# Attention stage of a two-block model: gate products ahead of modulation sums, a softmax in three parts with its maximum as ACT's bias, the output product in two halves, and two norms from one chain

## Chip, cores and metric

One NeuronCore of one Trainium2 chip runs the whole program. The metric is device time in microseconds (us) of the execution, lower is better.

## The reference

Two model blocks run one after the other on 256 tokens of 1024 channels, float32. The first (RWKV and mLSTM mixing, then a mixture of experts) ends in a norm; the second takes its result. The change lies where they meet and in the second block's attention:

```python
x = x + g_f * y                                   # end of block 1
x = rms_norm(x, final_norm_w)
# block 2, layer 0
mod = silu(c) @ w + b; shift, scale, gate = split(mod, 3)
h = rms_norm_2(x, norm_w) * (1.0 + scale) + shift
proj = h @ w_in                                   # gq gk gv gg glr sq sk sv
o_gla = gla_chunked(gq, gk, gv, log_a)            # 4 heads, chunks of 64
o_gla = rms_norm_2(o_gla, gla_norm_w) * silu(gg)
s = einsum(q, k) * 0.125 + bias                   # 8 heads, window 128, 2 blocks of 128 queries
m = maximum(max(s), sink)
p = exp(s - m); p = p / (sum(p) + exp(sink - m))
o_swa = einsum(p, v)
x = x + gate * (concatenate([o_gla, o_swa]) @ w_out)
# then norm, modulation and a squared-relu MLP of 4096; a second layer; final norm
```

`rms_norm(x, w)` is `x * rsqrt(mean(x*x) + 1e-6) * w`.

## The kernel before

The program is written engine by engine: each engine has one queue of instructions in the order of its function, and waits on counting semaphores. So the order of work around the change is the order in which the code is written. `Counter.link` lets an instruction count up a semaphore and then has its own engine wait for it; `mark` only counts up. The table `STEP` names counts, and `x.wait_ge(v["bs"], STEP["bs.sub0"])` waits for such a point (`v`, `a`, `g`, `t` are DVE, ACT, POOL and PE).

**Where block 1 ends.** `scatter` is the last expert product. DVE adds it to `x_sb` for each half of the tokens (`tt` 0 and 1, `v_residual`). Then for each half ACT squares and sums a row (L470), DVE makes the mean (L500), POOL raises it to the power -0.5 (L466) and DVE scales `x_sb` by root and weight (`final`, L2033). On the scaled row the same four steps are done again for block 2's norm, whose last one (L508) writes `xn`. PE transposes `xn` (L592), and DVE (L545) and ACT (L490) write the modulated `hT`. Then PE starts on the projections (L2699, the rank-16 gate).

**Projections and the gated linear attention.** `projection(0)` to `projection(8)` (L2687 to L2693) take 256 columns of `w_in` each, and 8 banks of PSUM are shared: projection i writes bank 6 + i % 2. Projections 4 and 5 give the output gate `gg`; ACT writes its sigmoid, and DVE multiplies it by the value still in the bank (L2098). `projection(6)` and `(7)` write the same two banks and wait for these two products. Between them PE makes the chunk states' sums (`bg.ds`, L2737) and the outputs (`bg.o`, L2749, L2752); DVE carries the state over the chunks in 12 small instructions (L2090, L2091).

**The modulation stream.** The vectors of the next modulation come from 24 pieces of `ada_w_2`, 0.5 MB each. SP loads piece n into one of four slots once DVE has used piece n - 4 (L745). `mod1_step` (L1165 for a vector's first piece, L1168) adds one piece to a sum on DVE. Pieces 0 to 7 make one vector, 8 to 15 the next, 16 to 23 the last; PE's `finish` sums over the partitions. Between the pieces SP also loads the four quarters of the output weight (L767, 1 MB each). All of it goes through one queue.

**Softmax and output.** PE makes the scores into six banks (L2770): two banks for the first 128 queries (`sc[:, :, 0:P]`), four for the second (two key blocks). DVE scales and adds the bias (L2134, L2141), and in `under_maximum` takes the maximum over a row (L2125), the maximum with the sink (L2126), their difference (L2127) and subtracts the maximum from all scores (L2128). ACT applies the exponential (L1515), PE transposes the weights (L2782), ACT copies them (L1519), PE multiplies by the values (L2789, L2791), DVE divides (L2155) into `y2`. PE transposes `y2` (L2801; channels 0 to 511 are the linear attention, 512 to 1023 the softmax attention), ACT copies a rounded part (L1539), DVE the rest (L578). The output product `mm3` (L573) then takes three passes for each product of 128x512: rounded by rounded, rounded by rest, rest by rounded. The weight is split in the same way: `out_hi_copy` (L1509) on ACT, `trailing` for the rest, its first three quarters on POOL (L1041), the fourth on DVE. After 96 products in four banks, block 2's next norm (`l0`) and the MLP follow.

## Time and profile before

| | |
|---|---|
| three runs, us | 1256.24, 1245.6, 1258.23 |
| median, us | 1256.24 |
| the profiled execution, us | 1254.31 |
| its span from first to last instruction, us | 1252.6 |
| busy share of the span: PE, DVE, ACT, POOL | 85%, 51%, 28%, 14% |
| mean granted clock of TensorE | 0.922 |

The busy shares are averages over stages with different limits. The change touches the stretch from 636 to 816 us of the profiled span, a seventh of it. There PE is the engine on which all others hang, and what is to be read is which wait of PE's ends last.

### The profile page before, as it was taken

Reading aid. Unit: us, or ns where it says so; the run is one execution under the profiler, and the core shown is the slowest. Engines: PE = TensorE matmul, PEld = TensorE weight load, DVE = VectorE, ACT = ScalarE, POOL = GpSimd, SP = SyncE. Lnnn points to the kernel's source line nnn. Section 1 sums busy time; section 2 is a strip of 40 time slices with the busy share of each in tenths; the row PEclk is TensorE's granted clock in tenths of the full one; section 3 lists DMA queues with packets and bytes.
Section 4 is the critical chain, followed back from the end, with each engine's and each line's share of the span. In section 5 each row is a group of like instructions: output and inputs, shape, how many; then the busy total and the mean of one; then the engine's idle time right before and its main releaser. Section 6 shows DMA issues by size and latency. Waiting matters only on the chain.

```text
span 1252.6 us, 16197 instructions
## 1 busy us (share of the span) xinstructions
PE 1070.0 (85%) x6588; PEld 814.6 (65%) x6588; DVE 640.0 (51%) x812; ACT 351.5 (28%) x440; POOL 178.0 (14%) x234
## 2 busy tenths in 40 slices
PE   1898977999978899999539794979999976999995
PEld 1787844997535455555227683858888865888884
DVE  6565567646444333323045727376757467553433
ACT  1130024241111111111023105166354315543531
POOL 4701013000200133231011004011111130000000
PEclk9998987999977999999869997889999977999998
DMA  9979638204679999999979703056676461545510
GB/s 352 351 163 307 242 123 305 102 1 169 228 305 408 383 401 353 356 339 355 407 226 371 277 1 135 1 203 251 235 294 225 134 247 73 192 144 194 225 67 34
DMA packets 114090, 287.48 MB, mean 230 GB/s; under 512 B 16406, under 2 KB 42334, under 8 KB 114026
## 3 DMA queue, kind: packets, MB, share of 16 engines
q1 hardware_dynamic: 94514, 245.45, 52.6%
q10 hardware_dynamic: 7560, 26.74, 6.3%
q0 software_dynamic: 11952, 14.38, 3.8%
q8 instruction: 46, 0.75, 0.2%
q14 instruction: 18, 0.15, 0.0%
HBM read 334.23 MB, written 2.62 MB: 269 GB/s over the span
## 4 chain that ended last, share of the span: by engine, by line
PE 68%; DMA 13%; DVE 10%; SPq 3%; ACT 2%; issue 2%; POOL 1%; DVEq 0%; ACTq 0%; POOLq 0%
PE ps L573 29%; PE ps L2245 6%; PE ps L2582 5%; DMA arena<-in_moe_w_down_dram 4%; PE ps L2561 4%; PE ps L2421 3%; DMA macc<-in_ada_w_dram 3%; PE ps L2609 3%; DMA ring<-in_w_in_dram 2%; PE ps L2508 2%; PE ps L2687 2%; SPq L763 1%; PE ps L2624 1%; DMA ring<-in_ada_w_dram 1%; SPq L619 1%
## 5 line engine op out<-in xcount | busy, mean ns | idle before, releaser
L578 DVE TENSOR_TENSOR ring_parts<-ring,arena_parts 128x2048 fp32r<-128x2048 f32 x65 | 146.6, 2286 | 49.1 <-ACT arena_parts L1109 42.1
L573 PE MATMUL ps<-arena_parts,macc_parts 128*128 128x512 f32 x512 | 166.0, 396 | 0.0
L573 PE MATMUL ps<-arena_parts,gate_parts 128*128 128x512 f32 x288 | 114.6, 398 | 8.3 <-DVE hT_parts L578 8.3
L573 PE MATMUL ps<-ring_parts,gate_parts 128*128 128x512 f32 x288 | 113.5, 394 | 0.0
L573 PE MATMUL ps<-arena_parts,hT_parts 128*128 128x512 f32 x288 | 113.4, 394 | 0.0
L573 PEld LDWEIGHTS ps<-arena_parts,macc_parts 128*128 128x128 f32 x512 | 96.2, 188 | 19.6
L573 PE MATMUL ps<-ring_parts,macc_parts 128*128 128x512 f32 x256 | 99.8, 390 | 0.0
L1109 ACT CAST arena_parts<-ring 128x2048 fp32r<-128x2048 f32 x32 | 60.3, 1908 | 84.5 <-DMA ring<-in_mlp_w_dram 43.4
L2245 PE MATMUL ps<-hT,ring 128*128 128x256 f32 x288 | 70.1, 409 | 5.6 <-DMA ring<-in_w_in_dram 5.6
L2245 PEld LDWEIGHTS ps<-hT,ring 128*128 128x128 f32 x288 | 59.5, 208 | 15.3 <-DMA ring<-in_w_in_dram 6.0
L573 PEld LDWEIGHTS ps<-arena_parts,gate_parts 128*128 128x128 f32 x288 | 55.1, 191 | 20.5 <-DVE hT_parts L578 9.1
L2582 PE MATMUL ps<-ring,hT 128*32 128x256 f32 x1024 | 61.7, 387 | 5.3 <-issue 3.4
L466 POOL TENSOR_TENSOR small<-small,nhalf 128x1 f32<-128x1 f32 x16 | 10.0, 625 | 390.1 <-DVE small L500 390.0
L573 PEld LDWEIGHTS ps<-arena_parts,hT_parts 128*128 128x128 f32 x288 | 55.0, 191 | 11.7
L573 PEld LDWEIGHTS ps<-ring_parts,gate_parts 128*128 128x128 f32 x288 | 55.1, 191 | 11.3
L1089 ACT CAST arena_parts<-ring 128x2048 fp32r<-128x2048 f32 x32 | 60.0, 1911 | 5.3 <-DMA ring<-in_mlp_w_dram 5.2
L578 DVE TENSOR_TENSOR macc_parts<-ps,macc_parts 128x512 fp32r<-128x512 f32 x32 | 22.1, 691 | 75.9 <-ACT macc_parts L1133 75.9
L2012 DVE SCALAR_TENSOR_TENSOR macc_parts<-ps,small,macc_parts 128x512 fp32r<-128x512 f32 x24 | 16.9, 747 | 85.8 <-ACT macc_parts L1439 85.8
L1572 DVE SCALAR_TENSOR_TENSOR macc<-ring,ccol,macc 128x1024 f32<-128x1024 f32 x42 | 54.0, 1285 | 8.5 <-DMA ring<-in_ada_w_dram 7.1
L2582 PEld LDWEIGHTS ps<-ring,hT 128*32 128x32 f32 x1024 | 34.3, 112 | 33.9 <-issue 13.5
L2609 PE MATMUL ps<-arena,gate 128*32 128x512 f32 x384 | 45.6, 607 | 10.8 <-DMA arena<-in_moe_w_down_dram 9.5
L573 PEld LDWEIGHTS ps<-ring_parts,macc_parts 128*128 128x128 f32 x256 | 48.2, 188 | 9.3
(539 smaller groups left out, 1799.0 us busy)
## 6 DMA issues: line engine op xcount, KB each, us to landing
ring<-in_mlp_w_dram SPq DMA_DIRECT2D x40, 1024.0 KB, 7.6
arena<-in_moe_w_down_dram SPq DMA_DIRECT2D x16, 2048.0 KB, 12.4
ring<-in_ada_w_dram SPq DMA_DIRECT2D x29, 1024.0 KB, 13.4
ring<-in_mlp_w_dram ACTq DMA_DIRECT2D x24, 1024.0 KB, 7.1
ring<-in_moe_w_up_dram SPq DMA_DIRECT2D x10, 2048.0 KB, 22.3
ring<-in_moe_w_gate_dram SPq DMA_DIRECT2D x10, 2048.0 KB, 17.8
arena<-in_ada_w_dram SPq DMA_DIRECT2D x15, 1024.0 KB, 7.0
ring<-in_w_in_dram SPq DMA_DIRECT2D x13, 1024.0 KB, 18.4
```

What stands on the lines that cost most here:

```text
L573: ins = nc.tensor.matmul(o, l, r, start=start and i == 0, stop=stop and i == 2, skip_group_check=True)
L578: return eng.tensor_tensor(lo, x, hi.bitcast(F32), ALU.subtract)
L1089: nc.scalar.copy(mlp_hi[s_], ring[:, s_, :]).then_inc(a_w2, 1)
L1109: nc.scalar.copy(mlp_hi[s_], ring[:, s_, :]).then_inc(a_w1, 1)
L1572: ins = nc.vector.scalar_tensor_tensor(acc, w[:, r, :], ccol[:, k:k + 1], acc, ALU.mult, ALU.add)
L2245: ins = nc.tensor.matmul(o, w[:, k, P * j:P * j + P], hT[:, k, :], start=k == 0, stop=k == KT - 1)
L2421: ins = nc.tensor.matmul(o, lhs[:, gi, hh], rhs[:, gi, hh], start=True, stop=True)
L2508: ins = nc.tensor.matmul(ps[:, 4 + j, :], hT[:, k, P * (j // 2):P * (j // 2) + P], w, start=k == 0, stop=k == KT - 1)
L2561: ins = nc.tensor.matmul(ps[:, 6 + i // 2, 256 * (i % 2):256 * (i % 2) + 256], xn[:, tt, P * k:P * k + P], picked[:, tt, :], start=tt == 0 ...
L2582: ins = nc.tensor.matmul(ps[rows, 4 + i % 2, FE * half:FE * half + FE], hT[:, k, P * (i % 2) + CAPQ * j:P * (i % 2) + CAPQ * j + CAPQ], w[ ...
L2609: ins = nc.tensor.matmul(ps[rows, 6 + h, :], tb[:, P * f + CAPQ * j:P * f + CAPQ * j + CAPQ], down_w[:, j, f, 512 * h:512 * h + 512], star ...
L2687: ins = nc.tensor.matmul(o, w[:, k, P * j:P * j + P], hT[:, k, :], start=k == 0, stop=k == KT - 1)
```

## The change

Five edits, engine by engine. `order` shows what each engine's queue holds; line numbers after the change are larger, up to 100 by the end.

**Norms.** Where block 1 meets block 2, `x_sb` is multiplied by the weight alone (`weighted`, into `xn`), and both sums of squares are taken beside each other, of `x_sb` and of `xn`. With v = mean(x²)+1e-6 and w2 = mean((x·w)²) the second norm's factor on x·w is (w2 + 1e-6·v)^-0.5, so that its chain does not need the root of v; that root is used for `x_sb` alone, whose scaling (`final_out`) now comes behind `hT`. POOL:

```diff
+g_rstd(pool, cn, "bn", 0)
+g_rstd(pool, cn, "bn", 1)
 for tt in range(TT):
-    g_rstd(pool, cf, "f", tt)
-    g_rstd(pool, cn, "bn", tt)
+    pool.wait_ge(v["f"], STEP[f"f.ss{tt}"])
+    cf.link(nc.gpsimd.tensor_tensor(f_var[tt], f_var[tt], nhalf[:, 0:1], ALU.pow))
+    cf.at(f"f.rstd{tt}")
```

The three subtractions of the weight's rest part leave POOL, and DVE has them behind the linear attention:

```diff
-for q in range(3):
-    pool.wait_ge(a["bs"], STEP[f"bs.hi{q}"])
-    c.link(trailing(nc.gpsimd, ring_lo[:, (9 + q) % RING, :], ring[:, (9 + q) % RING, :], out_hi[q]))
-c.at("bg.lo")
```

```diff
+for q in range(3):
+    dve.wait_ge(a["bs"], STEP[f"bs.hi{q}"])
+    c.link(trailing(nc.vector, ring_lo[:, (9 + q) % RING, :], ring[:, (9 + q) % RING, :], out_hi[q]))
+c.at("bg.lo")
```

ACT, the squares, and then its queue from projection 4 on:

```diff
-    a_square(cf, "f", tt)
-    act.wait_ge(v["f"], STEP[f"f.n{tt}"])
-    a_square(cn, "bn", tt)
+    cf.link(nc.scalar.activation(sq_out[tt], x_sb[:, tt, :], ACT.Square, accum_out=f_var[tt]))
+    cf.at(f"f.sq{tt}")
+    act.wait_ge(v["f"], STEP[f"f.w{tt}"])
+    cn.link(nc.scalar.activation(sq_out[tt], xn[:, tt, :], ACT.Square, accum_out=small[:, tt:tt + 1]))
+    cn.at(f"bn.sq{tt}")
...
 for i in range(4, 9):
     if i == 6:
         act.wait_ge(t_fin, FIN[1, 2])
     copied(i)
+    if i == 6:
+        act.wait_ge(t["bg"], STEP["bg.o"])
+        out_hi_copy(0)
+        act.wait_ge(v["bg"], STEP["bg.ss"])
+        out_hi_copy(1)
+    elif i == 7:
+        act.wait_ge(v["bg"], STEP["bg.y"])
+        out_hi_copy(2)
 cp.at("bp.a")
-
-c = Counter(act, a["bs"])
-
-def out_hi_copy(q):
-    act.wait_ge(ring2[(9 + q) % RING], 32)
-    c.link(nc.scalar.copy(out_hi[q], ring[:, (9 + q) % RING, :]))
-    c.at(f"bs.hi{q}")
+nc.scalar.activation(swm[:, 48:49], ones[:, 0:1], ACT.Exp)
 
 def exp_part(part):
     act.wait_ge(v["bs"], STEP[f"bs.sub{part}"])
-    s_ = sc[:, :, P * part:P + 2 * P * part]
-    c.link(nc.scalar.activation(s_, s_, ACT.Exp))
+    for i in range(8 if part == 0 else 4):
+        h = i + 4 * (part == 2)
+        s_ = sc[:, h, 0:P] if part == 0 else sc[:, h, P:3 * P]
+        m = i + (0, 8, 12)[part]
+        c.mark(nc.scalar.activation(s_, s_, ACT.Exp, bias=swm[:, m:m + 1]))
...
+ch = Counter(act, a["bo"])
+
+def out_t(k):
+    act.wait_ge(t["bo"], k // 2 + 1)
+    ch.link(nc.scalar.copy(gT_hi[:, k:k + 2, :], ps[:, k // 2, :].rearrange("p (k t) -> p k t", k=2)))
+
+for k in (0, 2):
+    out_t(k)
 exp_part(0)
-c.at("bs.exp0")
-for j in range(2):
+exp_part(1)
+for j in (0, 1):
     weights_t(j)
-out_hi_copy(2)
-exp_part(1)
+c.at("bs.pt0")
+exp_part(2)
 c.link(nc.scalar.activation(swm[:, 16:32], swm[:, 16:32], ACT.Exp))
-c.at("bs.exp1")
+c.at("bs.es")
 for j in range(2, 6):
     weights_t(j)
 c.at("bs.pt")
 out_hi_copy(3)
-c = Counter(act, a["bo"])
-for k in range(0, KT, 2):
-    act.wait_ge(t["bo"], k // 2 + 1)
-    c.link(nc.scalar.copy(gT_hi[:, k:k + 2, :], ps[:, k // 2, :].rearrange("p (k t) -> p k t", k=2)))
+for k in (4, 6):
+    out_t(k)
```

DVE's norms:

```diff
+def weighted(tt):
+    c.link(nc.vector.tensor_tensor(xn[:, tt, :], x_sb[:, tt, :], nrm_b, ALU.mult))
+    c.at(f"f.w{tt}")
+
+def final_var(tt):
+    dve.wait_ge(a["f"], STEP[f"f.sq{tt}"])
+    c.link(nc.vector.tensor_scalar(f_var[tt], f_var[tt], 1.0 / D, EPS, ALU.mult, ALU.add))
+    c.at(f"f.ss{tt}")
+    c.link(nc.vector.tensor_scalar(f_eps[tt], f_var[tt], EPS, None, ALU.mult))
+
+def both_var(tt):
+    dve.wait_ge(a["bn"], STEP[f"bn.sq{tt}"])
+    cn.link(nc.vector.scalar_tensor_tensor(small[:, tt:tt + 1], small[:, tt:tt + 1], 1.0 / D, f_eps[tt],
+                                           ALU.mult, ALU.add))
+    cn.at(f"bn.ss{tt}")
+
+def both_out(tt):
+    dve.wait_ge(g["bn"], STEP[f"bn.rstd{tt}"])
+    cn.link(nc.vector.tensor_scalar(xn[:, tt, :], xn[:, tt, :], small[:, tt:tt + 1], None, ALU.mult))
+    cn.at(f"bn.xn{tt}")
+
+def final_out(tt):
     dve.wait_ge(g["f"], STEP[f"f.rstd{tt}"])
-    c.link(nc.vector.scalar_tensor_tensor(x_sb[:, tt, :], x_sb[:, tt, :], small[:, tt:tt + 1], nrm_b,
-                                          ALU.mult, ALU.mult))
-    c.at(f"f.n{tt}")
+    c.link(nc.vector.scalar_tensor_tensor(x_sb[:, tt, :], x_sb[:, tt, :], f_var[tt], nrm_b, ALU.mult, ALU.mult))
...
-final(0)
+weighted(0)
+final_var(0)
 v_residual(dve, c, "f", gate1[:, 1, :], 0, 1, experts_of)
-v_mean(dve, cn, "bn", 0)
-v_mean(dve, c, "f", 1)
-v_xn(dve, cn, "bn", 0)
-final(1)
-v_mean(dve, cn, "bn", 1)
-v_xn(dve, cn, "bn", 1)
+weighted(1)
+both_var(0)
+final_var(1)
+both_out(0)
+both_var(1)
+both_out(1)
 v_norm_out(dve, cn, "bn", *mod_of[0])
+final_out(0)
+final_out(1)
+c.at("f.n1")
```

DVE's stream (the first `mod1_step` group of eight stays where it was):

```diff
-for n in range(8, 11):
-    mod1_step(dve, n)
...
-for n in range(11, 17):
+for n in range(8, 14):
     mod1_step(dve, n)
...
-for n in range(17, 24):
+for n in range(14, 19):
     mod1_step(dve, n)
...
 cp = Counter(dve, v["bp"])
 for i in (4, 5):
     dve.wait_ge(a["bp"], i + 1)
     gs = ggs[:, :, 256 * (i - 4):256 * (i - 4) + 256]
     cp.link(nc.vector.tensor_tensor(gs, gs, bin_bank(i).rearrange("p (a n) -> p a n", a=2), ALU.mult))
+for n in range(19, 24):
+    mod1_step(dve, n)
+
 dve.wait_ge(t["bg"], STEP["bg.o"])
```

DVE's softmax and the rest parts of `y2`:

```diff
+parts = ((0, sc[:, :, 0:P], 0), (8, sc[:, 0:4, P:3 * P], 0), (12, sc[:, 4:8, P:3 * P], 4))
+
+def under_maximum(o, s_, h0):
+    n = s_.shape[1]
+    m, e, s0 = mx[:, o:o + n], es[:, o:o + n], slice(h0, h0 + n)
+    c.link(nc.vector.tensor_reduce(m, s_, AX_X, ALU.max))
+    c.link(nc.vector.scalar_tensor_tensor(m, m, -1.0, nsink[:, s0], ALU.mult, ALU.min))
+    c.link(nc.vector.tensor_tensor(e, sink_b[:, s0], m, ALU.add))
 
...
+    if j % 2:
+        under_maximum(*parts[j // 2])
+        c.at(f"bs.sub{j // 2}")
...
+def out_lo(cb, k):
+    dve.wait_ge(a["bo"], k // 2 + 1)
+    cb.link(trailing(nc.vector, hT_lo[:, k:k + 2, :], ps[:, k // 2, :].rearrange("p (k t) -> p k t", k=2),
+                     gT_hi[:, k:k + 2, :]))
+
+cb = Counter(dve, v["bo"])
+for k in (0, 2):
+    out_lo(cb, k)
+dve.wait_ge(a["bs"], STEP["bs.es"])
+for o, s_ in ((0, sc[:, :, 0:P]), (8, sc[:, :, P:3 * P])):
     c.link(nc.vector.tensor_reduce(dn[:, o:o + 8], s_, AX_X, ALU.add))
...
-c = Counter(dve, v["bo"])
-for k in range(0, KT, 2):
-    dve.wait_ge(a["bo"], k // 2 + 1)
-    c.link(trailing(nc.vector, hT_lo[:, k:k + 2, :], ps[:, k // 2, :].rearrange("p (k t) -> p k t", k=2),
-                    gT_hi[:, k:k + 2, :]))
+c = cb
+for k in (4, 6):
+    out_lo(c, k)
```

PE from the scores on:

```diff
+def out_products(k0):
+    for j in range(4):
+        for k in range(k0, k0 + 4):
+            if j == 0 and k % 2 == 0:
+                pe.wait_ge(v["bo"], k // 2 + 1)
+            cols = slice(D * (k % 2) + 512 * (j % 2), D * (k % 2) + 512 * (j % 2) + 512)
+            tok = slice(P * (j // 2), P * (j // 2) + P)
+            ins = mm3(ps[:, 4 + j, :], gT_hi[:, k, tok], hT_lo[:, k, tok], out_hi[k // 2][:, cols],
+                      ring_lo[:, (9 + k // 2) % RING, cols], start=k == 0, stop=k == KT - 1)
+        if k0:
+            ins.then_inc(t_bout, 1)
+
+pe.wait_ge(v["bg"], STEP["bg.y"])
+out_transposes(0)
...
-    if j in (0, 2):
+    if j % 2 == 0:
         pe.wait_ge(a["bs"], STEP[f"bs.exp{j // 2}"])
...
+pe.wait_ge(a["bs"], STEP["bs.pt0"])
+for h in range(SWA_H):
+    kv = slice(64 * (h // 4), 64 * (h // 4) + 64)
+    ins = nc.tensor.matmul(ps[:, 2, 64 * h:64 * h + 64], p_t[:, h, :], svt[:, 0, kv], start=True, stop=True)
+c.mark(ins)
+c.at("bs.o0")
...
+pe.wait_ge(v["bg"], STEP["bg.lo"])
+out_products(0)
 pe.wait_ge(v["bs"], STEP["bs.y"])
+out_transposes(4)
+out_products(4)
```

DVE at the end of the chunk states. Before (L2090 and L2091 are the state, L2098 the gate products, L2101 to L2103 take the linear attention's output), and then after the change, where L2138 are the gate products and L1170 the stream's steps:

```order
L2090 TENSOR_TENSOR arena<-arena 64x2x128
L2091 TENSOR_TENSOR arena<-arena,ps 64x2x128
L2098 TENSOR_TENSOR arena<-arena,ps 128x2x256 x2
L2101 COPY macc<-ps 128x2x512
L2102 TENSOR_TENSOR arena<-macc 128x1024
L2103 TENSOR_REDUCE small<-arena 128x8
```

```order
L2131 TENSOR_TENSOR arena<-arena 64x2x128
L2132 TENSOR_TENSOR arena<-arena,ps 64x2x128
L2138 TENSOR_TENSOR arena<-arena,ps 128x2x256 x2
L1170 SCALAR_TENSOR_TENSOR wup<-gate,ccol,wup 128x1024
L1170 SCALAR_TENSOR_TENSOR wup<-macc,ccol,wup 128x1024 x2
L1170 SCALAR_TENSOR_TENSOR wup<-gate,ccol,wup 128x1024 x2
L2144 COPY macc<-ps 128x2x512
L2145 TENSOR_TENSOR arena<-macc 128x1024
```

Five steps of the stream, which stood ahead of the state, now stand behind the gate products.

PE from the scores (L2770, after it L2825) to the output product. Before, with the softmax's weights transposed in L2782, the products with the values in L2789 and L2791, and all of `y2` in L2801:

```order
L2770 MATMUL ps<-arena 128x128 x8
L2770 MATMUL ps<-arena 128x256 x8
L2782 MATMUL ps<-ident,arena 128x128 x24
L2789 MATMUL ps<-arena 128x64
L2791 MATMUL ps<-arena 128x64 x2
```

```order
L2791 MATMUL ps<-arena 128x64 x2
L2801 MATMUL ps<-ident,macc 128x128 x16
L573 MATMUL ps<-arena_parts,gate_parts 128x512
L573 MATMUL ps<-ring_parts,gate_parts 128x512
L573 MATMUL ps<-arena_parts,hT_parts 128x512
```

After it, with `y2` in L2836, the weights in L2860 and the values in L2867 and L2874:

```order
L2825 MATMUL ps<-arena 128x128 x8
L2825 MATMUL ps<-arena 128x256 x8
L2836 MATMUL ps<-ident,macc 128x128 x8
L2860 MATMUL ps<-ident,arena 128x128 x24
L2867 MATMUL ps<-arena 128x64 x8
L2874 MATMUL ps<-arena 128x64 x16
L576 MATMUL ps<-arena_parts,gate_parts 128x512
L576 MATMUL ps<-ring_parts,gate_parts 128x512
L576 MATMUL ps<-arena_parts,hT_parts 128x512
```

Half of the transposes of `y2` moved ahead of those of the softmax, and the output product's first half directly behind the products with the values; the other half of the transposes stands behind its 48th instruction.

ACT from projection 6 on. Before (L1464 and L1468 copy projections, L1509 rounds the weight, L1515 is the exponential, L1519 copies the transposed weights):

```order
L1464 COPY arena<-ps 128x512 x2
L1468 COPY arena<-ps 64x256 x4
L1469 COPY arena<-ps 128x256
L1509 CAST arena_parts<-ring 128x2048 x2
L1515 ACT_TABLE_LOAD
L1515 ACTIVATE arena<-arena 128x8x128
L1519 COPY arena<-ps 128x512 x2
L1509 CAST arena_parts<-ring 128x2048
L1515 ACTIVATE arena<-arena 128x8x256
```

After it (L1507 rounds the weight, L1531 is the exponential, L1542 copies the transposed `y2`):

```order
L1468 COPY arena<-ps 128x512
L1507 CAST arena_parts<-ring 128x2048 x2
L1468 COPY arena<-ps 128x512
L1507 CAST arena_parts<-ring 128x2048
L1472 COPY arena<-ps 64x256 x4
L1473 COPY arena<-ps 128x256
L1523 ACT_TABLE_LOAD
L1523 ACTIVATE arena<-ones 128x1
L1542 CAST gate_parts<-ps 128x512 x2
L1531 ACTIVATE arena<-arena 128x128 x8
L1531 ACTIVATE arena<-arena 128x256 x4
L1536 COPY arena<-ps 128x512 x2
```

Three roundings moved up between the copies of projections, the table load ahead of the softmax, and two instructions became sixteen, with two copies of `y2` ahead of them.

## Rows read from the trace of the kernel before

**Rows 1.** Windows: start:end, length, busy us per engine, PEclk, DMA share, GB/s.

```profile
684.00:711.00 27.00, 26.86 (x133) 22.34 (x131) 22.10 (x22) 4.92 (x8) 0.00 (x0) 1.00 0.98 376
776.00:790.00 14.00, 11.71 (x64) 11.12 (x64) 7.61 (x7) 4.24 (x5) 2.08 (x1) 0.62 0.00 0
790.00:816.00 26.00, 25.98 (x119) 22.16 (x120) 8.87 (x14) 4.01 (x7) 0.54 (x1) 0.93 0.00 1
```

**Rows 2.** Timeline of PE: start us, busy us, line, operation, idle before and releaser.

```profile
656.40 5.51 PE L2699 MATMUL ps<-hT,arena 128*16 128x256 f32 x16 [1.72 <-DVE hT L545]
...
703.68 7.17 PE L2689 MATMUL ps<-ring,hT 128*128 128x256 f32 x32
718.73 8.61 PE L2687 MATMUL ps<-hT,ring 128*128 128x256 f32 x32 [7.87 <-DVE arena L2098]
...
753.53 5.51 PE L2770 MATMUL ps<-arena 128*128 128x128 f32 x32 [2.11 <-ACT arena L1469]
...
780.40 0.43 PE L2789 MATMUL ps<-arena 128*128 128x64 f32 x2 [0.73 <-ACT arena L1519]
...
790.02 3.58 PE L2801 MATMUL ps<-ident,macc 128*128 128x128 f32 x16 [1.58 <-DVE macc L2155]
...
815.24 1.04 PE L592 MATMUL ps<-ident,arena 128*128 128x128 f32 x8
```

**Rows 3.** Timeline, the same columns: ACT in the two norms.

```profile
639.13 1.06 ACT L470 ACTIVATE arena<-x_sb 128x1024 f32<-128x1024 f32 x1 [6.91 <-DVE x_sb L517]
...
642.71 1.06 ACT L470 ACTIVATE arena<-x_sb 128x1024 f32<-128x1024 f32 x1 [2.42 <-DVE x_sb L2033]
...
645.61 1.06 ACT L470 ACTIVATE arena<-x_sb 128x1024 f32<-128x1024 f32 x1 [1.75 <-DVE x_sb L517]
...
649.69 1.06 ACT L470 ACTIVATE arena<-x_sb 128x1024 f32<-128x1024 f32 x1 [2.94 <-DVE x_sb L2033]
```

**Rows 4.** Timeline of DVE beside the modulation stream, 677 to 713 us.

```profile
677.61 1.42 DVE L2059 TENSOR_TENSOR_SCAN arena<-early,arena 128x256 f32<-128x256 f32 x2
...
698.39 0.75 DVE L1165 TENSOR_SCALAR wup<-macc,ccol 128x1024 f32<-128x1024 f32 x1 [2.48 <-DMA macc<-in_ada_w_dram]
...
711.26 1.28 DVE L1168 SCALAR_TENSOR_TENSOR wup<-gate,ccol,wup 128x1024 f32<-128x1024 f32 x1 [0.49 <-DMA gate<-in_ada_w_dram]
712.47 0.41 DVE L2090 TENSOR_TENSOR arena<-arena 64x256 f32<-64x256 f32 x1
```

**Rows 5.** Source line 745, the stream's pieces: from issue to landing.

```profile
DMA to landing us min/median/max: 3.7/6.5/11.5
```

**Rows 6.** Timeline of DVE and then POOL in the softmax.

```profile
754.82 0.69 DVE L2134 SCALAR_TENSOR_TENSOR arena<-ps,arena 128x512 f32<-128x512 f32 x1 [10.83 <-PE ps L2770]
...
756.41 1.22 DVE L2125 TENSOR_REDUCE arena<-arena 128x8 f32<-128x1024 f32 x1
757.67 2.44 DVE L2126 TENSOR_TENSOR arena<-arena 128x8 f32<-128x8 f32 x1
...
760.34 5.41 DVE L2128 TENSOR_TENSOR arena<-arena 128x1024 f32<-128x1024 f32 x1
...
771.00 0.17 DVE L2126 TENSOR_TENSOR arena<-arena 128x8 f32<-128x8 f32 x1
...
782.38 2.29 DVE L578 TENSOR_TENSOR ring_parts<-ring,arena_parts 128x2048 fp32r<-128x2048 f32 x1 [2.30 <-ACT arena_parts L1509]
...
755.55 9.12 POOL L578 TENSOR_TENSOR ring_parts<-ring,arena_parts 128x2048 fp32r<-128x2048 f32 x2 [17.44 <-ACT arena_parts L1509]
```

**Rows 7.** Timeline of ACT, gate bias, exponentials and copies.

```profile
670.17 0.98 ACT L1479 ACTIVATE arena<-ps,prm_c 128x256 f32<-128x256 f32 x2 [0.48 <-PE ps L2705]
...
765.83 1.28 ACT L1515 ACT_TABLE_LOAD   x1 [8.49 <-DVE arena L2128]
...
773.79 1.91 ACT L1515 ACTIVATE arena<-arena 128x2048 f32<-128x2048 f32 x1 [0.98 <-DVE arena L2128]
...
779.76 0.59 ACT L1519 COPY arena<-ps 128x512 f32<-128x512 f32 x1 [0.27 <-PE ps L2782]
```

77 lines of the change are left out of this document (28 added, 49 removed), and 4 rows, old and new, of the table STEP.

## Prediction

> **What bounds the kernel now.** The change touches 636 to 816 us, so I read first the windows of that stretch for PE's busy time and clock, then PE's timeline for its waits, and then, for each wait, the timeline of the engine that is named behind it. From 684 to 711 us PE is busy throughout, and the DMA queues move 376 GB/s at a share of 0.98 [rows 1]: here two things run level, PE's projections and the stream of modulation pieces. Projection 5 ends at 703.68 + 7.17 = 710.85, and projection 6 starts at 718.73, after 7.87 us of waiting for DVE's gate products [rows 2]. DVE had them late because its last stream step, which had to wait for its piece, started at 711.26 and the state and the products stand behind it [rows 4]. From the scores at 753.53 to the first value product at 780.40 lie 26.9 us, of which PE works some 11 (5.5 on the scores, 24 transposes at 0.224); in the rest it waits for DVE and ACT. The output product runs from 790.02 + 3.58 = 793.6 to 815.24, 21.6 us for 96 passes, 0.225 us each [rows 2]. Whatever brings the end of it forward brings the whole rest of the program forward, as all the MLP needs it.
>
> **Norms.** Before, 3.58 us lie between the first square and the next one on ACT (square, mean, root, scaling), which is also when DVE can go on to the second half [rows 3]. Now DVE multiplies by the weight beside the square (1024 columns, 1.22 us by the row of the reduction [rows 6], my stand-in) and needs two tiny instructions: about 1.6 us, 1.9 saved. In the second half the second square started 4.08 us after the first [rows 3]; now it starts 1.3 after it: 2.8 saved. Against that, PE is still at the first half's eight transposes (0.224 us each at the low clock [rows 2]) and DVE's small steps queue: 0.5 back. Sum 4.2 us: PE starts its first projection at 652.2 instead of 656.40 [rows 2]. The two scalings of `x_sb` are moved behind `hT`, in front of stream steps that wait for transfers, and cost nothing.
>
> **Gate products.** With the norms PE would be done with projection 5 at 710.85 − 4.2 = 706.65. DVE's side: its scan ended at 679.03 [rows 4], behind eight stream steps that set its time, so it is not earlier. Steps 8 to 13 follow, then the mask, 14 to 18, the state, the products. Piece 16 landed at 698.4, where DVE waited for it [rows 4]; two more pieces at 376 GB/s, 1.4 us each, put piece 18 at 701.2. It is requested once step 14 is through, by my count 696.7 (piece 13 landed near 691.4, counted back from 698.4 at 1.4 a piece and 2.8 for the weight quarter between; then the step of 1.3 [rows 4], four instructions of 512 columns at 0.65, the step again), 4.5 us ahead, which the shortest landing of 3.7 us allows [rows 5]. Step 18 ends at 702.5. From the start of the state at 712.47 to projection 6 at 718.73 were 6.3 us [rows 4, 2], so projection 6 starts at 708.7. PE waits 2.1 instead of 7.87 us, and the start is 10.0 earlier than before. Norms and this edit are not two sums: without the norms PE would come at 710.85, and the pair would give 7.9. The five later steps (6.4 us) lie beside projection 6 (8.61), while DVE has nothing else to do but wait for the chunk outputs behind it; PE asks for the sum only after projection 7.
>
> From projection 6 to the scores were 34.8 us [rows 2], nearly all PE's own work. The three roundings now lie there on ACT, 1.9 us each as the exponential of that width [rows 7], between copies that come one to a projection; the three subtractions lie on DVE, 3 × 2.29 = 6.9 us [rows 6], behind the linear attention and inside the 10.83 us in which DVE waited for scores [rows 6]. If that cover were gone they would cost up to 6.9. I take 34.8 again: scores at 743.5.
>
> **Softmax.** In time from the start of the scores (t). The reduction starts at 2.9 as before, 1.22 us, and two small instructions follow, 1.6 in all [rows 6]: the first maximum is out at 4.5, after two more banks (0.7 each) the second at 7.5, the third at 10.5. Before, DVE's last subtraction let ACT start at 773.79, at 20.3 [rows 7]. Of that difference, 6.5 us are two instructions drawn out while POOL ran: the maximum with the sink took 2.44 us where the same one later took 0.17, and the subtraction 5.41 us where 1024 columns take 1.2 [rows 6]. The Trainium skill (SBUF — State Buffer, Who interferes with whom) has it that a DVE instruction with two SBUF inputs and a GpSimd instruction that reads SBUF exclude each other for the whole instruction; the trace agrees, as POOL's two end at 764.67 and DVE's ends 1.1 us later, while the reduction beside them kept its 1.22.
>
> ACT: its queue now has two copies of `y2` ahead of the exponentials, and they wait for PE's eight transposes, which stand behind the scores (5.5 + 1.8). The exponentials start at 8.4 though their data stood ready at 4.5: a wait that the change adds. A 128-column exponential isn't in the trace; between a copy of 512 (0.59) and an exponential of 2048 (1.91) a column costs 0.86 ns, so 0.26 us for 128 and 0.37 for 256, and a bias operand at 256 columns came to 0.49 [rows 7]. I take 0.28 and 0.45, nearer the low end for the short ones since they aren't linked: 2.3, 1.8 and 1.8 us for the three parts; the bounds are 2.1 to 3.9 and 1.5 to 2.0. Then: part 1 done at 10.7, part 2 at 12.5, two copies of transposed weights to 13.7, part 3 at 15.6, PE's last transposes at 17.3, when the first value products can start. (Before: 26.9.) The saving is 9.6. The table load of 1.28 us [rows 7] is now ahead of the scores' end, hidden by them.
>
> The Trainium skill (ScalarE: Activation LUTs, What ACT_TABLE_LOAD costs) speaks against many short activations: with a pointer bias 280 ns and 0.833 ns per column each, 0.39 and 0.49 us here, less some overlap. Standing alone that is 7.0 us, where I have 5.9, and the sum below would end 1.1 us later; no run before shows these forms.
>
> **Value and output products.** Before, the value products took 8.04 us (780.40 to 788.44), division and transposes another 5.2 to 793.6 [rows 2]. Now the first half of the output product needs only the linear attention's `y2`, whose parts are ready by t = 14, and follows directly: the 5.2 us go, and division and the last weight part run beside it. What is late next is the second half: its transposes (8 × 0.13 by the last row [rows 2]) and a copy and a rest part before the first two blocks are ready, 1.04 + 0.9 = 1.9. Saving 3.2. Value products at 743.5 + 17.3 = 760.8, end 768.8; 48 passes to 779.7; second half from 781.6 to 792.4, against 815.24. The next norm's chain behind it stays: its first half has 5 us less cover, and I count 0.3 us at most for it and leave it out.
>
> **Sum.** 10.0 + 9.6 + 3.2 = 22.8 us. The profiled execution took 1254.31 (1.7 over its span of 1252.6), 1.9 under the median of 1256.24. 1254.3 − 22.8 = 1231.5. I say **1232**. Ends of the terms: 6.4 to 11.5 (stream late, or a warm clock in projection 6: 8.61 against 7.17), 7.5 to 10.5, and 0.2 to 5.8 for the products. There the clock counts: the mean was 0.62 in 776 to 790 [rows 1], and eight us at that mean would be 5.0 at the upper of its two levels and 10.0 at the lower.
>
> **Rivals.**
> *The stream runs dry* (0.12). Steps 14 and 15 stand later, and so do the requests for 18 and 19. If piece 18 takes the longest landing of 11.5 us instead of 4.5, projection 6 starts 7.0 later: 1238.5. For it: 16 pieces kept the queue full, at a share of 0.98. Against: a late request finds less ahead of it.
> *ACT is the new bound of the softmax* (0.13). Exponentials at their upper bounds (+2.0) and value products at the lower clock (+2.0): 1235.5. For it: seven us of exponentials where there were three, in the queue on which PE waits three times.
> *The drawn-out instructions are their own fault* (0.03), not POOL's: then the three short steps with the sink take 2.44 each, +6.8: 1238. The 0.17 speaks against it.
> *Warmer than thought* (0.07): projection 6 at 7.17 and value products in 5: 1227.
> *Slower than before* (0.03): fewer and shorter waits, but PE stays at 1.2 GHz from the scores through the output product: 96 passes twice as long, +21.6, value products +2.0, transposes +0.9, together 24.5: 1256, and above 1257 with the MLP's first passes. It decides from 22.8 us on, so nearly all the product must run low; against it, PEclk was 0.93 from 790 on, right after 3.6 us of transposes at the lower level [rows 1, 2].
> The forecast itself has 0.62. Within 1% is what a measurement of this kernel can't tell from no change, since its three runs lie 1% apart. Faster by over 1% (under 1243.7) is the forecast and nearly all of four rivals: 0.90. Slower by over 1% needs more than the fifth: 0.02. For 8 in 10 I go from the warm case less the runs' scatter to the dry stream plus it: 1224 to 1243.
>
> **What would show it.** In the changed profile: PE's wait before projection 6 is about 2 us and its start near 709; DVE's three maxima are each 1.2 and 0.2 us; POOL has nothing beside them; the value products start 17 us after the scores; the gap inside the output product is 2 us. I am wrong if the stream's share drops with projection 6 still waiting over 5 us, if exponentials take over 0.5 us each, or if the passes take 0.4 us instead of 0.225.

## The result, and the profile after the change

| | before | after |
|---|---|---|
| times, us | 1256.24, 1245.6, 1258.23, 1255.45 | 1224.45, 1221.15, 1225.17, 1226.24 |
| median, us | 1255.85 | 1224.81 |
| profiled execution, its span, us | 1254.31, 1252.6 | 1224.45, 1222.5 |
| mean granted clock | 0.922 | 0.928 |

The ratio is 0.976 (95% interval 0.9724 to 0.9797). The prediction was 1232 us, with a range of 1224 to 1243: the time lies inside it, 7 us under the value named and 0.8 us above the lower end. A second measurement (number 9) gave a median of 1223.18 of six, which is 0.8 us below that end.

The windows of the changed kernel (start:end, length, busy us of PE, PEld, DVE, ACT and POOL, PEclk, DMA share, GB/s). The first is the stretch of [rows 1] in which projections and stream run level; the other two begin 10 us after the scores start.

```profile
677.00:704.00 27.00, 27.00 (x135) 22.79 (x134) 20.91 (x27) 7.02 (x10) 0.00 (x0) 1.00 0.99 377
750.00:754.00 4.00, 3.47 (x16) 2.73 (x16) 2.20 (x5) 3.94 (x10) 0.00 (x0) 0.57 0.17 69
754.00:784.00 30.00, 28.59 (x157) 24.60 (x158) 13.19 (x16) 6.95 (x11) 0.54 (x1) 1.00 0.00 1
```

The stream is as full as before (0.99, 377 GB/s). New is the third row: PEclk 1.00 through value products and output product, where 776 to 790 us had 0.62 and the stretch behind it 0.93 [rows 1]. PE's timeline (start us, busy us, line, operation, idle before and its releaser):

```profile
650.24 5.30 PE L2754 MATMUL ps<-hT,arena 128*16 128x256 f32 x16 [1.98 <-DVE hT L548]
...
697.32 7.17 PE L2744 MATMUL ps<-ring,hT 128*128 128x256 f32 x32
...
740.19 5.51 PE L2825 MATMUL ps<-arena 128*128 128x128 f32 x32 [2.11 <-ACT arena L1473]
...
749.90 3.56 PE L2860 MATMUL ps<-ident,arena 128*128 128x128 f32 x16 [3.33 <-ACT arena L1531]
754.32 1.10 PE L2860 MATMUL ps<-ident,arena 128*128 128x128 f32 x8 [0.85 <-ACT arena L1531]
755.26 1.90 PE L2867 MATMUL ps<-arena 128*128 128x64 f32 x16
756.99 3.74 PE L2874 MATMUL ps<-arena 128*128 128x64 f32 x32
...
771.54 1.04 PE L2836 MATMUL ps<-ident,macc 128*128 128x128 f32 x8
773.67 0.53 PE L576 MATMUL ps<-arena_parts,gate_parts 128*128 128x512 f32 x1 [1.09 <-DVE hT_parts L581]
...
784.75 1.03 PE L595 MATMUL ps<-ident,arena 128*128 128x128 f32 x8
```

These answer to [rows 2]. Projection 5 still ends at its own time (697.32 + 7.17 = 704.5), and projection 6 starts at 706.84, 2.35 us later instead of 7.87. From the scores to the first value product are 15.1 us instead of 26.9; the value products (1.90 + 3.74, overlapping: 5.47) follow, and the output product directly behind them, with one gap of 2.13 us between its halves (771.54 to 773.67), in which PE transposes the second half of `y2` and waits 1.09 us. DVE, same columns, to be read against [rows 4] and [rows 6]:

```profile
699.37 1.28 DVE L1170 SCALAR_TENSOR_TENSOR wup<-gate,ccol,wup 128x1024 f32<-128x1024 f32 x1 [0.82 <-DMA gate<-in_ada_w_dram]
700.57 0.41 DVE L2131 TENSOR_TENSOR arena<-arena 64x256 f32<-64x256 f32 x1
...
706.01 1.41 DVE L2138 TENSOR_TENSOR arena<-arena,ps 128x512 f32<-128x512 f32 x2
...
743.07 1.22 DVE L2175 TENSOR_REDUCE arena<-arena 128x8 f32<-128x1024 f32 x1
744.33 0.17 DVE L2176 SCALAR_TENSOR_TENSOR arena<-arena 128x8 f32<-128x8 f32 x1
...
750.72 0.16 DVE L2177 TENSOR_TENSOR arena<-arena 128x4 f32<-128x4 f32 x1
```

The state starts at 700.57, behind piece 18, for which DVE waited 0.82 us. The small steps with the sink take 0.17 and 0.16, where one took 2.44 and a subtraction 5.41. ACT, to be read against [rows 7], and POOL's operations on either side of the softmax:

```profile
746.17 1.20 ACT L1542 CAST gate_parts<-ps 128x512 fp32r<-128x512 f32 x2 [4.52 <-PE ps L2836]
747.40 4.04 ACT L1531 ACTIVATE arena<-arena 128x128 f32<-128x128 f32 x12
751.35 1.18 ACT L1536 COPY arena<-ps 128x512 f32<-128x512 f32 x2
752.57 1.71 ACT L1531 ACTIVATE arena<-arena 128x256 f32<-128x256 f32 x4
```

```profile
723.01 1.68 POOL L1043 TENSOR_TENSOR small<-small,nhalf 128x8 f32<-128x8 f32 x1 [66.07 <-DVE small L2147]
782.64 0.54 POOL L469 TENSOR_TENSOR small<-small,nhalf 128x1 f32<-128x1 f32 x1 [57.95 <-DVE small L503]
```

POOL has nothing between 724.7 and 782.6. ACT copies the output transposes first and starts the exponentials at 747.40, 7.2 us after the scores, although the first maximum was out at 744.7; four of 256 columns take 1.71.

**Where 30.1 us of the two profiled spans went.** 1.9 lie ahead of the change: the first residual addition stands at 634.35 and stood at 636.23. From there to projection 6 are 72.5 us instead of 82.5: 10.0. From projection 6 to the scores 33.35 instead of 34.80: 1.45, all of it projection 6 itself (7.14 instead of 8.61 us). From the scores to the end of the output product 44.56 instead of 61.71: 17.15. From there on, nothing (0.1 gained to the first MLP product, 0.5 lost behind it).

### The profile page after: what moved, and what is told of

Same layout as the page of the kernel before. It is cut to its first block, busy times and chain, and to the rows that moved or that the text cites. A ratio compares the mean times of both kernels' runs of the same rounds, so it can differ in the third digit from the quotient of the medians.

```text
span 1222.5 us, 16217 instructions
## 1 busy us (share of the span) xinstructions
PE 1065.5 (87%) x6588; PEld 809.9 (66%) x6588; DVE 639.8 (52%) x821; ACT 354.7 (29%) x455; POOL 163.4 (13%) x231
## 4 chain that ended last, share of the span: by engine, by line
PE 70%; DMA 10%; DVE 10%; SPq 3%; ACT 2%; issue 2%; POOL 2%; DVEq 0%; ACTq 0%; POOLq 0%
PE ps L576 30%; PE ps L2637 6%; PE ps L2300 6%; PE ps L2616 4%; DMA arena<-in_moe_w_down_dram 3%; PE ps L2476 3%; PE ps L2664 3%; DMA ring<-in_w_in_dram 3%; PE ps L2563 2%; PE ps L2742 2%; PE ps L2679 2%; SPq L766 1%; DMA ring<-in_ada_w_dram 1%; DMA macc<-in_ada_w_dram 1%; PE ps L1223 1%
## 5 line engine op out<-in xcount | busy, mean ns | idle before, releaser
L581 DVE TENSOR_TENSOR ring_parts<-ring,arena_parts 128x2048 fp32r<-128x2048 f32 x68 | 153.5, 2287 | 49.1 <-ACT arena_parts L1111 43.2
L576 PEld LDWEIGHTS ps<-arena_parts,hT_parts 128*128 128x128 f32 x288 | 55.1, 191 | 11.8
```

The lines of the kernel that those rows point to most:

```text
L576: ins = nc.tensor.matmul(o, l, r, start=start and i == 0, stop=stop and i == 2, skip_group_check=True)
L581: return eng.tensor_tensor(lo, x, hi.bitcast(F32), ALU.subtract)
```

## Experiments

Distances below are counted in each kernel's own trace, since the starting point itself (the first residual addition) moves between 630 and 639 us from one execution to the next. The times of the kernel before on the same chips lay at medians of 1251.7 to 1255.9. The stage from the scores to the end of the output product is called the last stage. The upper and the lower level are TensorE's granted clock of 1.00 and 0.50 (2.4 and 1.2 GHz). Each variant has one profile and four to ten times. The 95% interval of every variant of the changed kernel overlaps at least one of the changed kernel's own two (0.9724 to 0.9797, and 0.9763 to 0.9834 in number 9), so the totals alone decide little; the readings below rest on positions in the traces.

**1. Norms put back** (the changed kernel with ACT's, DVE's and POOL's code of the two norms as before).

```diff
-cf.link(nc.scalar.activation(sq_out[tt], x_sb[:, tt, :], ACT.Square, accum_out=f_var[tt]))
-act.wait_ge(v["f"], STEP[f"f.w{tt}"])
+a_square(cf, "f", tt)
+act.wait_ge(v["f"], STEP[f"f.n{tt}"])
...
-final_out(0)
-final_out(1)
```

> The changed kernel with only the norms as they were before (two chains, one behind the other). Theory (two paths meet at projection 6, the later one sets it; the stream of modulation pieces sets DVE's path): PE comes to projection 6 about 4.3 us later, the gate products are as early as with the new norms, so PE's wait there falls from 2.35 us to 0 and the start is about 2 us later, counted from the first residual addition; total +2 us against the changed kernel, about 1227. Rival (the norms are a term of their own): +4.3 us, wait still 2.3 us, about 1229.

Median 1228.26 (1220.8 to 1231.76), ratio 0.9782 (0.9718 to 0.9847). PE, projections 5 and 6:

```profile
697.74 7.17 PE L2717 MATMUL ps<-ring,hT 128*128 128x256 f32 x32
704.75 7.07 PE L2715 MATMUL ps<-hT,ring 128*128 128x256 f32 x32
```

There is no wait any more: 74.5 us from the residual addition instead of 72.5. Norms worth 4.3 us at PE's first projection are worth 2.0 at projection 6, because without them PE comes later than DVE. This is the expected 2 us with no wait left; the total of 1228.26 can't tell 2 us from the rival's 4.3. The two edits act on two paths that meet, and the later one decides.

**2. Stream steps put back** (three of them stand again ahead of the exponentials' use, none behind the gate products).

```diff
+for n in range(8, 11):
+    mod1_step(dve, n)
...
-for n in range(8, 14):
+for n in range(11, 17):
...
-for n in range(14, 19):
+for n in range(17, 24):
...
-for n in range(19, 24):
-    mod1_step(dve, n)
```

> The changed kernel with only the modulation steps back where they were (8 to 10 ahead of the decay, 11 to 16, 17 to 23 ahead of the chunk state). Theory (the stream sets DVE's path and so swallows the norms' gain as well): projection 6 starts where it started before the change, 82.5 us after the first residual addition against 72.5, PE waits 12 us there; total +10 us and 1.5 more where a long wait brings projection 6 to the lower clock, about 1236. Rival (terms add up): +5.7 us, about 1230.5, with a wait of 8 us.

Median 1241.1 (1232.61 to 1243.61), ratio 0.9882 (0.9814 to 0.9951). PE's projection 6 and DVE ahead of it:

```profile
716.60 8.83 PE L2741 MATMUL ps<-hT,ring 128*128 128x256 f32 x32 [4.09 <-DVE arena L2140]
```

```profile
707.72 2.71 DVE L1170 SCALAR_TENSOR_TENSOR wup<-gate,ccol,wup 128x1024 f32<-128x1024 f32 x2 [0.38 <-DMA gate<-in_ada_w_dram]
...
715.77 1.41 DVE L2140 TENSOR_TENSOR arena<-arena,ps 128x512 f32<-128x512 f32 x2
```

Projection 6 starts 81.6 us after the residual addition, 9.1 later (expected were 10), and runs at the lower clock besides. The wait in front of it is 4.09 us and not the 12 expected, since PE had already waited 2.06 us ahead of the score products of the linear attention (L2773) and 3.38 us ahead of the chunk sums (L2791), and ran projection 5 at the lower clock (9.15 instead of 7.17 us). The last stream step is done only at 710.4, as the stream brings its piece: with the old order the faster norms gain under 1 us. So the norms alone were worth nearly nothing, and the pair 10. The median is 5 us above the 1236 expected; the last stage of this profile, 53.31 us, has the lower clock too.

**3. Stream order alone, in the kernel before** (the same lines as in 2, the other way).

> The kernel before with only the modulation steps moved behind the gate products. Theory: PE arrives at projection 6 as before, 74.6 us after the first residual addition, and waits under 0.5 us: 7.9 us earlier than before, and projection 6 at the upper clock takes 7.15 instead of 8.6: 9 us in all, about 1246 to 1247. Rival (the gain is the 5.8 us by which the wait shrank in the changed kernel): 5.8 us, about 1250.

Median 1247.23 of ten (1238.27 to 1252.9), ratio 0.995 (0.9911 to 0.9989).

```profile
702.60 7.17 PE L2689 MATMUL ps<-ring,hT 128*128 128x256 f32 x32
709.62 7.07 PE L2687 MATMUL ps<-hT,ring 128*128 128x256 f32 x32
```

Projection 6 starts without a wait 74.1 us after the residual addition, 8.4 earlier (expected 7.9), and takes 7.07 us instead of 8.61: 9.9 in all, where 9 were expected. In this execution the clock stayed up in the projections behind it as well, so that the scores came 11.6 us earlier; but the median gained only 5.5 us on the kernel before (0.5%), which is nearer the rival's 5.8 than the 9 expected; this profile (1239.35) is at the fast end of its ten times. The trace decides for the theory: the wait is gone altogether by the step order alone.

**4. Output product in one piece** (transposes and products of all eight blocks behind the softmax's `y2`; ACT's and DVE's parts with them).

```diff
-for k in range(k0, k0 + 4):
+for k in range(k0, 8):
...
-pe.wait_ge(v["bg"], STEP["bg.y"])
-out_transposes(0)
...
+pe.wait_ge(v["bs"], STEP["bs.y"])
+out_transposes(0)
 pe.wait_ge(v["bg"], STEP["bg.lo"])
 out_products(0)
-pe.wait_ge(v["bs"], STEP["bs.y"])
-out_transposes(4)
-out_products(4)
```

> The changed kernel with the output product in one piece again: all sixteen transposes of y2 and their copies behind the division, 96 passes behind them. Theory (the split is half paid for by the wait that it adds on ACT): from the end of the value products to the last pass 26 to 27 us instead of 24.2, but the exponentials start at 4.5 us from the scores instead of 7.2, and the value products about 1.5 us earlier; net +0.5 to +1.5 us. Rival (the split saves what the prediction gave it, 3.2 us, and ACT's copies hinder nobody): +3.2 us or more.

Median 1232.32 (1231.87 to 1234.98), ratio 0.9842 (0.9784 to 0.99).

```profile
747.80 1.10 PE L2853 MATMUL ps<-ident,arena 128*128 128x128 f32 x8 [1.53 <-ACT arena L1531]
...
754.25 3.52 PE L2860 MATMUL ps<-arena 128*128 128x64 f32 x16
757.56 7.03 PE L2867 MATMUL ps<-arena 128*128 128x64 f32 x32
765.80 3.67 PE L2832 MATMUL ps<-ident,macc 128*128 128x128 f32 x16 [1.21 <-DVE macc L2208]
```

```profile
758.00:770.00 12.00, 10.79 (x49) 10.51 (x50) 5.53 (x6) 2.19 (x4) 0.00 (x0) 0.50 0.00 1
```

Expected were 0.5 to 1.5 us more, and the median is 7.5 us above the first four of the changed kernel. A gap of 4.5 us between value products and output product is back (764.59 to 769.12), but the exponentials start at 4.5 us instead of 7.2, since no copies stand ahead of them, and the value products at 13.5 instead of 15.1. What made the last stage 6.7 us longer (51.25 instead of 44.56) is mostly what the second fence shows: PE at the lower level, at work for 10.8 of 12 us, and value products of 10.34 us instead of 5.47. The granted clock was 0.50 for 17 us from 13.5 us after the scores (3.4 us in the changed kernel); below this is called the long fall. This run alone can't say what the split is worth; number 5 says more.

**5. First exponentials ahead of the copies** (ACT's queue).

```diff
+exp_part(0)
 for k in (0, 2):
     out_t(k)
-exp_part(0)
 exp_part(1)
```

> The changed kernel with ACT's first eight exponentials ahead of the two copies of the transposed y2, nothing else moved. Theory (the copies make the exponentials wait though their data is ready at 4.5 us from the scores): exponentials start at 4.5 instead of 7.2 us, the value products at 13.5 to 13.8 instead of 15.1, total 1.3 to 1.5 us less. Rival (DVE's last maximum at 10.5 us or PE's transposes set the end anyway): no change within 0.3 us.

Median 1231.06 (1226.72 to 1236.28), ratio 0.9843 (0.9757 to 0.9929). The first exponential started at 4.5, the value products at 14.4, 0.6 us earlier than in the changed kernel though the last transposes now took 1.97 us, at the lower level. Then value products of 10.34 us and an output product of 26.64: last stage 51.18. Expected were 1.3 to 1.5 us less in all, which this variant did not give. Beside number 4 (51.25) the split output product gains 0.1 us net. From the start of the value products on it is 1.0 us faster (36.74 and 37.77): the gap of 4.5 us is filled by products, but they run at half speed, and the gap of 2.13 us between the halves is new. Ahead of them it is 1.0 us later, of which 0.8 are the last transposes, at the lower level here and at the upper in number 4; so the two profiles don't price the split exactly.

**6. Subtraction back on DVE** (one exponential for each part, no bias).

```diff
-    c.mark(nc.scalar.activation(s_, s_, ACT.Exp, bias=swm[:, m:m + 1]))
...
+c.mark(nc.scalar.activation(s_, s_, ACT.Exp))
...
+c.link(nc.vector.tensor_tensor(s_, s_, m.unsqueeze(2).to_broadcast([P, n, s_.shape[2]]), ALU.add))
```

> The changed kernel with the maximum subtracted on DVE and one exponential for each of the three parts, in place of sixteen exponentials with the maximum as bias. Theory (the bias form moves 3.7 us of subtractions from DVE to some 3 us of extra ACT time, and DVE is the later of the two): third part ready at 14.3 instead of 10.5 us from the scores, exponential 1.06 us, value products at 17 instead of 15.1: +2 us. Rival (ACT is the bound, sixteen instructions cost more than they save): value products earlier, 1 us or more less.

Median 1234.43 (1231.84 to 1238.21), ratio 0.9878 (0.9798 to 0.9959). DVE:

```profile
745.18 1.22 DVE L2175 TENSOR_TENSOR arena<-arena 128x1024 f32<-128x1024 f32 x1
```

Three of these lie on the path; the value products start at 17.4 us instead of 15.1, where 17 was expected. Of the 2.4 us, 0.8 are clock (last transposes of 1.97 instead of 1.10) and 1.5 are the form: the third exponential ends at 15.6 instead of 14.1.

**7. Two rest parts back on POOL, beside the softmax.**

```diff
+pool.wait_ge(t["bs"], STEP["bs.s0"])
+for q in range(2):
+    pool.wait_ge(a["bs"], STEP[f"bs.hi{q}"])
+    c.link(trailing(nc.gpsimd, ring_lo[:, (9 + q) % RING, :], ring[:, (9 + q) % RING, :], out_hi[q]))
...
-for q in range(3):
+for q in (2,):
```

> The changed kernel with two of the three subtractions for the weight's rest part back on POOL, started with the first bank of scores, so that they run beside DVE's maxima. Theory (a DVE instruction with two inputs in SBUF waits for a POOL instruction that reads SBUF): two of DVE's small instructions with the maxima, 0.17 us each now, take up to 4 us, the reductions (one input) stay at 1.22; third maximum 4 to 8 us later; total +4 to +6 us. Rival (the 2.44 and 5.41 us of before were the instructions' own): the small ones stay at 0.17, total unchanged within 1 us.

Median 1227.44 (1226.86 to 1231.75), ratio 0.9811 (0.9732 to 0.9889). DVE and POOL:

```profile
742.94 1.22 DVE L2180 TENSOR_REDUCE arena<-arena 128x8 f32<-128x1024 f32 x1
744.19 1.70 DVE L2181 SCALAR_TENSOR_TENSOR arena<-arena 128x8 f32<-128x8 f32 x1
...
748.84 1.67 DVE L2181 SCALAR_TENSOR_TENSOR arena<-arena 128x4 f32<-128x4 f32 x1
...
753.43 0.16 DVE L2181 SCALAR_TENSOR_TENSOR arena<-arena 128x4 f32<-128x4 f32 x1
```

```profile
741.35 9.13 POOL L581 TENSOR_TENSOR ring_parts<-ring,arena_parts 128x2048 fp32r<-128x2048 f32 x2 [16.79 <-issue]
```

POOL's two end near 745.9 and at 750.48, DVE's two long steps at 745.89 and 750.51: an instruction of DVE on eight elements a row waits until POOL's has ended. The same one takes 0.16 once POOL is done, and the reductions, with one input, keep their 1.22. That costs 3.0 us of DVE time. The value products start at 17.4 us, 2.3 later, but only 1.5 of that is POOL's doing (the third part's exponentials start at 13.8 instead of 12.4); 0.8 are the last transposes at the lower clock. Expected were 4 to 6 us: the subtraction that suffered most before (5.41 us) no longer exists, and a wait ends with POOL's instruction, so it is long only for who comes early in it. This profile (1231.75, with a last stage of 52.75 us and value products of 10.3) is also over 4 us above the variant's three other times (1226.86, 1227.44, 1227.44).

**8. The kernel before, with PE's idle time partly filled** by bf16 products of zeros that nothing reads: 20 ahead of the scores, 88 and 56 ahead of the first and the third group of transposes.

```diff
+def filler(n):
+    for i in range(n):
+        nc.tensor.matmul(ps[:, 0, P * (i % 4):P * (i % 4) + P], zeros_b, zeros_b, start=True, stop=True,
+                         skip_group_check=True)
```

> The kernel before with idle-time fillers on PE: 20, 88 and 56 bf16 products of 128x128 on zeros into an unused bank, ahead of the scores and of the two groups of transposes of the softmax weights; nothing else changed. Theory (5 to 6 us of the measured gain over the forecast are the granted clock, because PE idles less there): transposes 24 in 3.2 instead of 5.6 us where they aren't hidden, value products 5.4 instead of 8.0 us, transposes of y2 2.1 instead of 3.6 us; total 4 to 6 us less than before. Rival (the clock there doesn't follow what PE did before): no change, or slower by the fillers.

Median 1252.36 of ten (1249.26 to 1260.59), ratio 1.0001 (0.9963 to 1.0038).

```profile
763.96 5.08 PE L2763 MATMUL ps<-zeros_b 128*128 128x128 bf16 x88
773.34 1.97 PE L2790 MATMUL ps<-ident,arena 128*128 128x128 f32 x8 [4.30 <-ACT arena L1515]
775.10 3.75 PE L2763 MATMUL ps<-zeros_b 128*128 128x128 bf16 x56
781.11 1.97 PE L2790 MATMUL ps<-ident,arena 128*128 128x128 f32 x16 [2.26 <-ACT arena L1530]
```

No gain, where 4 to 6 us were expected. This looks like a refutation of the idea that idling costs the clock, but the rows say less: gaps of 4.30 and 2.26 us were left open. The granted clock was 1.00 for 14 us from the start of the scores, fell to 0.50 inside the first of these gaps for 3.4 us, and again in the middle of the value products, for 13.6 us. Numbers 11 and 12 close the gaps.

**9. The changed kernel again,** a second profile and five more times.

> The changed kernel, not edited: a second profiled execution of it and five more rounds of times. Open after the runs so far: from the scores to the end of the output product, the profiled execution of the changed kernel had the upper clock level in almost every 4 us window (value products 5.47 us), while all its variants had granted clock 0.50 for some 16 us there (value products 10.34 us). Theory one, the clock there is drawn anew in each execution: the value products of this profile may take anything from 5.5 to 10.4 us, the span goes with it (1222 to 1230 us), and the median stays within 1222 to 1229. Theory two, the order of instructions of the changed kernel itself keeps the clock up: value products again 5.5 us and the value products' start again about 15 us after the scores. In either, the first exponential starts 8.4 us after the scores, projection 6 starts 72.5 us after the first residual addition, and projection 6 waits some 2.3 us.

Median 1223.18 (1221.2, 1222.92, 1222.96, 1223.4, 1224.79 and one of 1233.82), ratio 0.9798 (0.9763 to 0.9834). The same two windows as above, from 10 us after the scores:

```profile
747.00:751.00 4.00, 3.48 (x16) 3.12 (x16) 2.19 (x5) 3.92 (x10) 0.00 (x0) 0.59 0.16 62
751.00:781.00 30.00, 28.59 (x157) 24.60 (x158) 13.19 (x16) 6.94 (x11) 0.54 (x1) 1.00 0.00 1
```

The second profile repeats the first: value products 5.48 us, start at 15.1, last stage 44.57, first exponential at 7.2 (the 8.4 of the expectation was the prediction's number). Projection 6 starts 72.4 us after the residual addition again (after a wait of 3.98, as PE was earlier), but it ran at the lower level (8.83 us). Nine of ten executions of the changed kernel lie between 1221.1 and 1226.3, the tenth 8 us above. All six variants so far (1, 2, 4 to 7), whose profiles show the long fall, are at medians of 1227 to 1241. So an even draw in each execution (theory one) doesn't fit, and theory two, the order, fits with an exception now and then. But the order isn't all of it. Number 1 has the changed kernel's instructions in this stage and had the long fall (its scores, other than the changed kernel's, ran at the lower level for their first 3.5 us), and within one variant the times lie as far apart as the two lengths of the fall would put them: 1231.76 (profiled) and 1220.8 in number 1, 1231.75 (profiled) and 1226.86 in number 7, 1231.1 (profiled) and 1219.88 in number 10. The granted clock of this stage is known only for the profiled ones, so that the length varies between executions of one kernel is likely, and not shown.

**10. Three edits for speed:** number 5; two of the MLP's first weight pieces loaded once the output product's first half is through; the first rest part ahead of the second half's mean.

```diff
+sp.wait_ge(t_win, 14)
+first_chunks_in(sp, 0, (1, 2))
 sp.wait_ge(t_bout, 4)
-first_chunks_in(sp, 0, (1, 2, 3, 4))
+first_chunks_in(sp, 0, (3, 4))
...
+if tt and mod:
+    mod(cn)
 v_mean(dve, cn, nst, tt)
```

> The changed kernel with three edits more: the first exponentials stand ahead of ACT's copies of output transposes; two of the four slots that the output product's first half frees are loaded with the MLP's first pieces while its second half still runs; and in both norms that end in an MLP, DVE makes the first weight piece's trailing part ahead of the second half's mean, where it waits for nothing. Theory: the first exponential starts 4.5 us after the scores, the value products start some 1 us earlier than in an execution of the changed kernel at the same clock, ACT no longer waits for a DMA ahead of the MLP's first matmuls (2.24 us before them in the changed kernel), and the stretch from the last output product to the first MLP matmul falls from 11.05 us to about 9.5; the norm ahead of the second MLP gains as much, so the time is 2 to 3 us under that of the changed kernel on the same chip. Rival: the wait for the DMA was hidden behind the norm, and the trailing part moved ahead delays the mean by its own 2 us: the stretch stays at 11 us or grows by 1, and the time stays within 1 us of the changed kernel's.

Median 1229.2 (1219.88 to 1234.43), ratio 0.9818 (0.978 to 0.9855). ACT and DVE at the norm:

```profile
795.31 1.90 ACT L1115 CAST arena_parts<-ring 128x2048 fp32r<-128x2048 f32 x1
```

```profile
794.16 2.29 DVE L583 TENSOR_TENSOR ring_parts<-ring,arena_parts 128x2048 fp32r<-128x2048 f32 x1
796.37 0.15 DVE L503 TENSOR_SCALAR small<-small 128x1 f32<-128x1 f32 x1
```

ACT's wait for the DMA is gone, as meant, and the stretch to the first MLP product is still 11.04 us (11.05 before the edit): the rest part fills a wait of 1.3 us and delays the mean by the 1 us that is left over, and PE's transposes come after 5.2 us of waiting instead of 4.2. The rival was right about the stretch. Its second half, a time within 1 us of the changed kernel's, did not come (1229.2 against 1223.18 on the same chip): the last stage took 51.18, with the long fall.

**11 and 12. Idle stretches filled.** Number 11 is the changed kernel with fillers of 30, 52 and 14; number 12 has number 5's exchange too, and fillers of 30, 10, 28 and 14, placed where PE waits for ACT.

```diff
+pe.wait_ge(v["bg"], STEP["bg.y"])
+filler(30, 0)
 pe.wait_ge(a["bp"], STEP["bp.a"])
...
 if j % 2 == 0:
+    pe.wait_ge(v["bs"], STEP[f"bs.sub{j // 2}"])
+    filler((52, 0, 14)[j // 2], bs_bank[j])
     pe.wait_ge(a["bs"], STEP[f"bs.exp{j // 2}"])
```

> The changed kernel with PE's idle stretches of this stage filled by small bf16 products of zeros that nothing reads: 30 of them ahead of the scores (PE idles 2.11 us there in the changed kernel), 52 between the output transposes and the first transposes of the weights (3.33 us idle), 14 ahead of the last ones (0.85 us idle); one took 0.06 us in the run of the kernel before with such fillers. Theory: the granted clock falls to 0.5 some 10 us after the scores start because PE idled at 6 to 9 us after them; where PE has work there it stays at 1.0, the transposes stay at 1.0 to 1.1 us for eight, the value products at 5.5 us, and the times gather at 1220 to 1225 us with none like the single 1233.8 of the changed kernel. Rival one: the clock falls as before for 3 us or for 16 us and by the same chances, the time is that of the changed kernel (1223 to 1226 us median). Rival two: the fillers make it fall longer or later, in the value products and the output product, and the time is 5 to 8 us above the changed kernel's (1230 us).

> The same fillers in counts of 30, 10, 28 and 14, in the changed kernel with the first exponentials ahead of ACT's copies of output transposes. Theory: the first exponential starts 4.5 us after the scores, PE idles nowhere for more than 1 us up to the value products, the clock stays up, the value products start at some 13.7 us instead of 15.1 and take 5.5 us, and the time is about 1.4 us under that of the filled kernel without the exchange, 1219 to 1223 us. Rival: the clock falls for 16 us as in the unfilled kernel with this exchange, the value products take 10.3 us, and the time is 1229 to 1231 us.

Number 11: median 1223.88 of six (1220.52 to 1225.86), ratio 0.9756 (0.9728 to 0.9784). Number 12: median 1221.21 of six (1217.97 to 1223.85), ratio 0.9726 (0.9697 to 0.9756), the fastest version here; its ratio is clear of number 9's (from 0.9763), measured on the same chip, but not of the changed kernel's first (from 0.9724). The same 4 us in number 5, then the windows of number 12, and its PE:

```profile
749.00:753.00 4.00, 1.97 (x8) 1.57 (x8) 3.72 (x7) 3.94 (x10) 0.00 (x0) 0.63 0.61 244
```

```profile
749.00:753.00 4.00, 3.45 (x51) 3.07 (x48) 3.79 (x7) 3.94 (x9) 0.00 (x0) 1.00 0.63 250
753.00:784.00 31.00, 29.35 (x161) 25.20 (x162) 13.98 (x19) 7.18 (x12) 0.54 (x1) 1.00 0.01 1
```

```profile
748.85 1.73 PE L2818 MATMUL ps<-zeros_b 128*128 128x128 bf16 x28
750.75 1.09 PE L2869 MATMUL ps<-ident,arena 128*128 128x128 f32 x8 [0.17 <-ACT arena L1531]
751.67 0.94 PE L2818 MATMUL ps<-zeros_b 128*128 128x128 bf16 x14
...
754.50 1.90 PE L2876 MATMUL ps<-arena 128*128 128x64 f32 x16
```

The same 4 us that had 0.57 in the changed kernel and 0.63 in number 5 now have 1.00, and all the stage behind them. Numbers 5 and 12 differ by the fillers alone: last stage 51.18 and 43.04, medians 1231.06 and 1221.21 (of different chips, with the kernel before at 1255.23 and 1254.71). That is 8 us of clock between these two profiles, bought with products of zeros. The times agree: of ten executions with the exchange and without fillers (numbers 5 and 10, the latter with two more edits) nine took 1226.7 us or more and one 1219.88, of the six with fillers none took over 1223.85. For number 11 the fillers are worth nothing against the changed kernel's usual execution (stage 44.51 and 44.56), and none of its six times is a high one; six don't prove that none will be. From 11 to 12 the stage falls by 1.47 us, which is what the exchange of ACT's first exponentials is worth at the upper clock; the medians fall by 2.7, their intervals overlap. In both the clock fell again behind the stage, in the next norm.

## Why the prediction held, step by step

**Norms, 4.2.** Measured 4.3 at PE's first projection (6.16 less the 1.88 that lay ahead); 2.0 of it counts at projection 6, and that it doesn't add to the next term was said and is shown by numbers 1 and 2.

**Gate products.** Forecast: wait 2.1, start 10.0 earlier, the pair worth 7.9 without the norms. Measured: 2.35, 10.0, and without the norms 8.0 in number 1 and 8.4 in number 3. The five steps behind the gate products cost nothing: PE takes up the sum behind projection 7 (L2688, 725.63) without a wait. The rival of the dry stream is out: DVE waited 0.82 us for piece 18.

**Projection 6 to the scores, 34.8.** 33.35: the projection ran at the upper level. In the second profile it was 35.04, at the lower. This 1.5 us is scatter, which the range had.

**Softmax, 9.6; measured 11.8.** The maxima were out at 4.5, 7.6 and 10.7 us against a forecast of 4.5, 7.5 and 10.5, POOL was absent, and the exponentials took 2.45, 1.71 and 1.71 (the first as a group of its own in number 12's order) against 2.3, 1.8 and 1.8. The estimate worked out from the Trainium skill (ScalarE: Activation LUTs, What ACT_TABLE_LOAD costs), 7.0 us in all where 5.9 came out, is that of instructions standing alone; in a row they took less. What was mis-sized is what hangs on the clock: the exponentials started at 7.2 instead of 8.4, since PE's output transposes took 1.04 us instead of 1.8, and the last transposes 1.1 instead of 1.7. POOL's part of the gain was real; beside the bias form it is smaller than the 6.5 us I read from [rows 6]: number 7 puts 3.0 on DVE and 1.5 on the path, as the bias form had already taken away the instruction that suffered most. The bias form is worth 1.5 by number 6. How the rest of the 11.8 divides between the three parts instead of two and the table load (1.28 us between maximum and exponential before [rows 7], now begun at 740.15 under the scores) was not tested.

**Value products, 8.04 kept.** This step failed: "the value products took 8.04 us" was carried over as if it were a property of the work. It is one clock or the other: 5.5 us in five profiles (the two of the changed kernel, numbers 3, 11 and 12), 10.34 in seven, and 8.04 is a mixture, as the 8.8 of number 8. The warmer rival, with 0.07, named this and priced it at 1227, and its conditions are what the profile shows (projection 6 in 7.14, value products in 5.47). With the transposes of the softmax the clock of the last stage makes some 4 us.

**Split output product, 3.2.** Gone are 5.1 us, back came 2.3 (gap 2.13): 2.8. That holds at the upper clock. At the lower one numbers 4 and 5 show 1.0 us from the value products on and nearly nothing net, which the prediction didn't see.

**Sum.** 22.8 forecast; 28.2 measured behind the first residual addition. Of the 5.4 between them, 1.45 are projection 6, 2.2 the softmax, 2.6 the value products, −0.4 the split and −0.4 the rest behind. TensorE's clock accounts for some 5.4 (projection 6, the value products, and 1.4 of the softmax); the rest cancels. The other 1.9 us, of the 7 by which the prediction was too high, lie ahead of the change, where the starting point moves from one execution to the next: they are scatter and no merit. So the paths and waits were right, and the number lay inside the range at its lower end because the clock term was mis-sized in the way that the warmer rival describes. The case that the new exponentials bound the stage (0.13) did not come as put: they were never at their upper prices, but its other condition, value products at the lower clock, is what seven of the variants' profiles show. The case slower than before was priced from the other end of the same mechanism; with the long fall the changed kernel would by its last stage still be over 20 us faster, as number 5 is (1231.06 against 1255.23).

What stays open is why the fall lasts 3.4 us in both profiles of the changed kernel and 17 to 21 in those of nearly identical ones. Two profiles show that it doesn't come where PE's gaps are filled; nothing here shows what decides its length where they are not.

## What to carry to other kernels

Where two edits shorten two paths that meet at one instruction, price them as a pair and once singly: here 4.3 and 8.4 made 10.0. Ahead of short matmuls, look at what PE did in the waits before them, not only at how long it waited: with the same order of work the stage took 43 us with its waits filled by products of zeros and 51 without (numbers 12 and 5), while the changed kernel's own order took 44.5 both ways, and filling only part of the waits gained nothing (number 8). Don't put GpSimd work with SBUF inputs beside a chain of tiny DVE steps; a step with two SBUF inputs pays for the rest of GpSimd's instruction (1.7 us instead of 0.16).

## What the runs showed of the hardware

- The granted clock fell from 1.00 to 0.50 (2.4 to 1.2 GHz) 9 to 14 us after the scores began in all twelve profiles whose waits stood open, wholly or in part (before, after, numbers 1 to 10); what PE had done there was to idle for 3.3 us in the changed kernel, for 1.5, 1.3 and 2.1 us in number 4, for 4.3 us in number 8. In the two whose waits were filled it stayed at 1.00 to the end of the output product. It was back after 3.4 us in both profiles of the changed kernel and at the first fall of number 8, after 17 us in the kernel before and numbers 3, 4 and 10, and after 20.5 us in numbers 1, 2, 5, 6 and 7, although PE was at work most of a long stretch of it (10.8 of 12 us in number 4).
- A value product of 64 columns costs 0.11 us (5.47 / 48) at the upper level and 0.215 (10.34 / 48) at the lower: 1.9 times as long at half the clock, as eight transposes are (1.04 to 1.10 against 1.97).
- The Trainium skill (SBUF — State Buffer, Who interferes with whom) says that a DVE instruction with two SBUF inputs and a GpSimd one that reads SBUF exclude each other. Number 7 agrees to 0.1 us: 1.70 and 1.67 us for steps of 0.17 and 0.16, each ending with POOL's, and 1.22 unchanged for the one-input reduction. The two-input step right behind the first of these (745.93, between POOL's two instructions) took 0.17.
- Exponentials with a bias operand in a row take 0.31 us for 128 columns (2.45 / 8) and 0.43 for 256 (1.71 / 4).
